# A gather-and-accumulate loop: every fourth expert value row is weighted and added on VectorE instead of on TensorE

## What is computed

```
u = take(w_u, expert)                       # [token, 128, 1024]
h = einsum('cd,ced->ce', x, u)              # one dot product of 1024 for each expert
a = gelu(h) * gate
y = einsum('ce,ced->cd', a, take(w_v, expert))   # weighted sum of 128 value rows
```

## Time and profile before

| what | value |
|---|---|
| time, median of 3 runs (lowest, highest) | 3867.13 us (3861.45, 3872.97) |
| profiled execution, first to last instruction | 3889.2 us |
| TensorE busy | 3225.7 us (83%) |
| VectorE busy | 2469.6 us (64%) |
| GpSimd busy | 2306.0 us (59%) |
| ScalarE busy | 471.7 us (12%) |
| HBM read / written | 1222.33 MB / 15.73 MB |
| mean granted TensorE clock | 0.973 |

### The profile page before, as it was taken

One profiled execution on the slowest core, in us unless ns is written; L12 is line 12 of the kernel. 1 busy time (PEld: TensorE's weight loads), 2 busy tenths in 40 slices (PEclk: granted clock), 3 DMA queues, 4 the chain that ended last, 5 costly groups with the idle time before them and its releaser, 6 DMA issues.

```text
span 3889.2 us, 35666 instructions
## 1 busy us (share of the span) xinstructions
PE 3225.7 (83%) x9848; PEld 1705.4 (44%) x9848; DVE 2469.6 (64%) x5900; ACT 471.7 (12%) x810; POOL 2306.0 (59%) x2075
## 2 busy tenths in 40 slices
PE   6999968698899887798999886887998986766676
PEld 3456744254564453354564552344664542222222
DVE  5143068478776677578765686577665885577654
ACT  1121011021111110021110010121111110000000
POOL 4000017765666767766566667655667667776775
PEclk9999989999999999999999999998999999999999
DMA  4135449998999999998999999988999999999998
GB/s 169 77 103 168 152 158 349 358 342 305 344 385 382 373 359 348 353 335 303 358 379 378 366 344 348 356 318 307 369 380 375 384 336 353 364 343 346 327 365 301
DMA packets 350437, 1240.65 MB, mean 319 GB/s; under 512 B 38480, under 2 KB 46160, under 8 KB 349712
## 3 DMA queue, kind: packets, MB, share of 16 engines
q0 software_dynamic: 294912, 1073.87, 74.7%
q1 hardware_dynamic: 34096, 117.94, 8.3%
q10 hardware_dynamic: 21216, 46.40, 3.4%
HBM read 1222.33 MB, written 15.73 MB: 318 GB/s over the span
## 4 chain that ended last, share of the span: by engine, by line
PE 40%; DMA 19%; issue 14%; DVE 12%; POOL 8%; DVEq 6%; another core or an unknown queue 1%; ACT 0%; POOLq 0%; SPq 0%
PE acc L592 17%; DMA rows<-in_peer_v,ids_peer 14%; PE fA L513 5%; DMA rows<-in_peer_u,ids_peer 5%; POOL rows L299 4%; POOL rows L309 4%; PE fB L525 3%; DVE rows L853 3%; DVE diag L864 2%; PE fA L473 2%; PE m L361 2%; PE m L557 1%; PE acc L579 1%; PE fA L536 1%; PE fB L536 1%
## 5 line engine op out<-in xcount | busy, mean ns | idle before, releaser
L592 PE MATMUL acc<-rows,diag 128*128 128x512 f32 x4096 | 1995.6, 620 | 539.2 <-DMA rows<-in_peer_v,ids_peer 468.7
L853 DVE CUSTOM_DVE_ANT_0 rows<-rows,hh 128x1024 f32<-128x1024 f32 x1024 | 1240.4, 1222 | 711.9 <-DMA rows<-in_peer_u,ids_peer 657.7
L299 POOL DMA_INDIRECT rows<-in_peer_u,ids_peer x1024 | 1108.4, 1082 | 889.9 <-DVE ids_peer L833 351.0
L309 POOL DMA_INDIRECT rows<-in_peer_v,ids_peer x1024 | 1149.5, 1123 | 534.5 <-issue 284.0
L592 PEld LDWEIGHTS acc<-rows,diag 128*128 128x128 f32 x4096 | 745.6, 194 | 1570.5 <-DMA rows<-in_peer_v,ids_peer 790.8
L864 DVE TENSOR_SCALAR diag<-ident,act_out,gate_peer 128x128 f32<-128x128 f32 x1024 | 283.6, 366 | 0.5 <-ACT act_out L1072 0.5
L557 PE MATMUL m<-hT_g,wring 128*128 128x256 f32 x1024 | 237.4, 386 | 1.1 <-ACT hT_g L1043 1.1
L513 PE MATMUL fA<-hT_g,wring 128*128 128x256 f32 x1024 | 231.2, 380 | 0.0
L557 PEld LDWEIGHTS m<-hT_g,wring 128*128 128x128 f32 x1024 | 198.9, 195 | 55.4 <-issue 29.1
L513 PEld LDWEIGHTS fA<-hT_g,wring 128*128 128x128 f32 x1024 | 195.3, 191 | 47.2 <-issue 23.0
L1072 ACT ACTIVATE act_out<-dots 128x8 f32<-128x8 f32 x128 | 26.7, 209 | 1052.5 <-DVE dots L853 705.5
(11 more groups left out here) (149 smaller groups left out, 2072.3 us busy)
## 6 DMA issues: line engine op xcount, KB each, us to landing
wring<-in_wstream SPq DMA_DIRECT2D x192, 512.0 KB
ln<-in_dft_seq ACTq DMA_DIRECT2D x32, 512.0 KB, 3.7
rows<-in_peer_u,ids_peer POOLq DMA_INDIRECT x1024
rows<-in_peer_v,ids_peer POOLq DMA_INDIRECT x1024
hT_g<-in_x SPq DMA_DIRECT2D x8, 512.0 KB, 3.7
hres_spill<-KT ACTq DMA_DIRECT2D x8, 512.0 KB, 2.7
hT_spill<-rows ACTq DMA_DIRECT2D x1, 4096.0 KB
wring<-in_wstream SPq DMA_DIRECT2D x16, 256.0 KB
```

Source lines behind the costliest of these rows:

```text
L299: pool.indirect_dma_start(u_rows[:, i % NU, :], None, peer_u, bass.IndirectOffsetOnAxis(ap=ids_peer[:, t, s:s + 1], axis=0)).then_inc(u_in ...
L309: pool.indirect_dma_start(v_rows[:, i % NV, :], None, peer_v, bass.IndirectOffsetOnAxis(ap=ids_peer[:, t, s:s + 1], axis=0)).then_inc(v_in ...
L592: last = mm(acc[:, half * 512:(half + 1) * 512], diag[:, i % NDIAG, :], v_rows[:, i % NV, half * 512:(half + 1) * 512], start=i % SLOTS == ...
L853: v.tensor_tensor_reduce(out=row, in0=row, in1=h1_peer[:, t, :], scale=1.0, scalar=0.0, op0=ALU.mult, op1=ALU.add, accum_out=dots[:, b, i ...
```

## The change

Of every four slots, the last one (slot number mod 4 equal to 3, which is always the fourth buffer of the v ring) no longer goes to TensorE. VectorE waits for its row to land and adds coefficient times row to an SBUF tile `yvec`; the first such slot of a tile writes `yvec` instead of adding. The coefficients (activation times gate) of a batch's two such slots come from one small multiplication in `diags`, which writes six diagonal matrices instead of eight. GpSimd's v gather of such a slot waits on a semaphore of VectorE (`v_added`) instead of TensorE's. `finish` adds `yvec` to the tile's result with one more instruction after it has freed `acc`.

```diff
+VEC = 4
+PE_BATCH = BATCH - BATCH // VEC
+PE_STEPS = STEPS - STEPS // VEC
...
             def gather_v(g, i):
                 g, i = slot_of(g, i)
-                pool.wait_ge(v_free, g * STEPS + i + 1 + NDIAG - NV)
+                if i % VEC == VEC - 1:
+                    pool.wait_ge(v_added, g * (STEPS // VEC) + i // VEC + 1)
+                else:
+                    pool.wait_ge(v_free, g * PE_STEPS + pe_slots(i) + 1)
...
                 if i % SLOTS == 0:
                     pe.wait_ge(acc_free, g * TILES + i // SLOTS + 1)
+                if i % VEC == VEC - 1:
+                    return
                 if i % BATCH == 0:
-                    pe.wait_ge(diag_done, g * STEPS + i + BATCH)
+                    pe.wait_ge(diag_done, g * PE_STEPS + pe_slots(i) + PE_BATCH)
...
+            def add_row(g, i):
+                g, i = slot_of(g, i)
+                if i % VEC != VEC - 1:
+                    return
+                dve.wait_ge(v_in[i % NV], g * (16 * STEPS // NV) + 16 * (i // NV + 1))
+                c = coef[:, i // BATCH % 2, i % BATCH // VEC:i % BATCH // VEC + 1]
+                if i % SLOTS == VEC - 1:
+                    v.tensor_scalar(yvec[:, :], v_rows[:, i % NV, :], c, None, ALU.mult).then_inc(v_added, 1)
+                else:
+                    v.scalar_tensor_tensor(out=yvec[:, :], in0=v_rows[:, i % NV, :], scalar=c, in1=yvec[:, :],
+                                           op0=ALU.mult, op1=ALU.add).then_inc(v_added, 1)
...
-                dve.wait_ge(v_free, g * STEPS + BATCH * k + BATCH)
+                if positive(g * PE_STEPS + PE_BATCH * (k - 1)):
+                    dve.wait_ge(v_free, NV - 1 + g * PE_STEPS + PE_BATCH * (k - 1))
                 t, s0 = divmod(k * BATCH, SLOTS)
+                v.tensor_tensor(coef[:, k % 2, :], act_out[:, k % 2, VEC - 1:BATCH:VEC],
+                                gate_peer[:, t, s0 + VEC - 1:s0 + BATCH:VEC], ALU.mult)
                 for s in range(BATCH):
-                    v.tensor_scalar(diag[:, (k * BATCH + s) % NDIAG, :], ident[:, :], act_out[:, k % 2, s:s + 1],
+                    if s % VEC == VEC - 1:
+                        continue
+                    v.tensor_scalar(diag[:, pe_slots(k * BATCH + s) % (2 * PE_BATCH), :], ident[:, :], act_out[:, k % 2, s:s + 1],
                                     gate_peer[:, t, s0 + s:s0 + s + 1], ALU.mult, ALU.mult).then_inc(diag_done, 1)
...
                                        op0=ALU.mult, op1=ALU.add).then_inc(acc_free, 1)
+                dve.drain()
+                v.tensor_tensor(ybuf[:, :], ybuf[:, :], yvec[:, :], ALU.add)
...
             def peer(g, m, last):
                 if has_slot(g, m + LEAD + AHEAD, last):
                     dot(g, m + LEAD + AHEAD)
+                if has_slot(g, m + LEAD, last):
+                    add_row(g, m + LEAD)
```

More of the change, by code:

```diff
@@ L44 @@
 NDIAG = 2 * BATCH
+VEC = 4
+PE_BATCH = BATCH - BATCH // VEC
+PE_STEPS = STEPS - STEPS // VEC
+assert NV == VEC
 NW = 4
@@ L95, in layer_program @@
         hT_g = sb("hT_g", [P, KD, GROUP])
-        diag = sb("diag", [P, NDIAG, P])
+        diag = sb("diag", [P, 2 * PE_BATCH, P])
         ln = sb("ln", [P, 4, D])
@@ L104, in layer_program @@
         ybuf = sb("ybuf", [P, D])
+        yvec = sb("yvec", [P, D])
         ident = sb("ident", [P, P])
@@ L128, in layer_program @@
         act_out = sb("act_out", [P, 2, BATCH])
+        coef = sb("coef", [P, 2, BATCH // VEC])
         st = sb("st", [P, 3, 12])
@@ L212, in layer_program @@
         v_in = [sem(f"v_landed{i}") for i in range(NV)]
-        u_free, v_free, acc_free = sem("u_free"), sem("v_free"), sem("acc_free")
+        u_free, v_free, v_added, acc_free = sem("u_free"), sem("v_free"), sem("v_added"), sem("acc_free")
         act_done, diag_done = sem("act_done"), sem("diag_done")
@@ L232, in has_slot, with pe_slots @@
             return i < STEPS and not (isinstance(g, int) and g < 0) or i >= STEPS and not last
+        def pe_slots(i):
+            return i - i // VEC
         def used(g, c):
@@ L331, in tr @@
                 return nc.tensor.transpose(out_, in_, ident[:, :])
-            for _ in range(NDIAG):
+            for _ in range(NV - 1):
                 pe.nop().then_inc(v_free, 1)
@@ L587, in peer @@
                     pe.wait_ge(acc_free, g * TILES + i // SLOTS + 1)
+                if i % VEC == VEC - 1:
+                    return
                 if i % BATCH == 0:
-                    pe.wait_ge(diag_done, g * STEPS + i + BATCH)
+                    pe.wait_ge(diag_done, g * PE_STEPS + pe_slots(i) + PE_BATCH)
                 pe.wait_ge(v_in[i % NV], g * (16 * STEPS // NV) + 16 * (i // NV + 1))
                 for half in range(2):
-                    last = mm(acc[:, half * 512:(half + 1) * 512], diag[:, i % NDIAG, :],
+                    last = mm(acc[:, half * 512:(half + 1) * 512], diag[:, pe_slots(i) % (2 * PE_BATCH), :],
                               v_rows[:, i % NV, half * 512:(half + 1) * 512],
-                              start=i % SLOTS == 0, stop=i % SLOTS == SLOTS - 1)
+                              start=i % SLOTS == 0, stop=i % SLOTS == SLOTS - 2)
                 last.then_inc(v_free, 1)
@@ L634, in _ @@
                 dve.nop().then_inc(u_free, 1)
+            dve.nop().then_inc(v_added, 1)
             dve.nop().then_inc(acc_free, 1)
@@ L870, in finish @@
                 dve.wait_ge(stored, 16 * (g * TILES + t) + 16)
-                dve.wait_ge(v_free, g * STEPS + NDIAG + (t + 1) * SLOTS)
+                dve.wait_ge(v_free, g * PE_STEPS + NV - 1 + (t + 1) * pe_slots(SLOTS))
                 v.scalar_tensor_tensor(out=ybuf[:, :], in0=h1_peer[:, t, :], scalar=ALPHA, in1=acc[:, :],
                                        op0=ALU.mult, op1=ALU.add).then_inc(acc_free, 1)
+                dve.drain()
+                v.tensor_tensor(ybuf[:, :], ybuf[:, :], yvec[:, :], ALU.add)
                 dve.drain()
```

## The result

The changed kernel takes 3900.52 us in the median (3893.46 to 3910.36), the kernel before 3870.05 us in the runs beside it. The two medians are 30 us apart; the ratio of the runs, by which all kernels are compared here, is 1.0097, interval 1.0053 to 1.0141, so 38 us slower (21 to 55), where 24 us faster was forecast.

A forecast was written before the change was run, and what follows sets the result against it. TensorE was taken to pace gate, merge and output alone and share attention, with transfers near their limit and GpSimd's gathers filling the rest; -30 - 10 + 5 + 14 + 0 - 3 = -24 from 3867 gives 3843 us, range 3795 to 3915.

The forecast's parts named there:

- Which stages TensorE sets: TensorE alone sets the pace in gate, merge and output, shares it in attention, and doesn't in about 60% of slots.
- What it removes and adds: Whole kernel: TensorE 440 us less; VectorE about 270 us more net, with adds taken at 1.25 us each.
- Gate, merge and output, 30 us gained: These stages in three groups: gate step falls from 3.47 to 3.28 us, transfers then limit; 30 us gained, ends 7 and 60.
- What of VectorE's work lies on the path: Stage by stage, VectorE's added work mostly hidden: 5 us lost in attention with retrieval, 14 in top-k, nothing without front work.
- attention with retrieval: Attention beside the second tile's retrieval: TensorE's relief and VectorE's burden nearly cancel, 5 us lost; ends 25 lost, 30 gained.
- top-k: First tile's top-k, steps 157 to 221: added rows mostly hidden in waits for u rows, 14 us lost, ends 0 and 60.
- steps without front work: Steps after the query projections and the last group: nothing gained or lost, slot again 2.99 us.
- idle, so covered: Steps without front work: VectorE's 37% idle in the last group covers the added work and its waits for value rows.
- Rival 3: Attention with retrieval and top-k: VectorE becomes the bound, its late lumps stopping GpSimd's gathers; 3895 to 3919 us, chance 0.20.
- the point that I set for it: Rival 3 decides once the net 1.0 us of VectorE's work per added row finds no wait to fill.
- The adds hold up GpSimd: Rival 4, where GpSimd is 95% occupied: each add delays a gather by up to 1.25 us; 3948, half 3895; chance 0.05.
- 30 + 10 + 3 us: Gains booked: 30 us in gate, merge and output, 10 in attention's first part, 3 net at the end.

The follow-up runs named there:

- x_pe_frees: Changed kernel, but TensorE frees every fourth slot's buffer without matmul and VectorE neither waits nor adds (that part of the sum left out): 3825.19 us, ratio 0.9909.
- xf_filler: x_pe_frees with two zero-matrix matmuls on TensorE in place of every fourth slot's work: 3817.49 us, ratio 0.9893 of the kernel before.
- g_gate: Kernel before, with VectorE adding only the 16 rows a group due in the gate, merge and output stages (steps 72 to 135): 3868.20 against 3888.62 us, ratio 0.9952.
- y_dve_waits: Changed kernel, but VectorE only waits for every fourth slot's row and frees the buffer, without adding: 3840.33 us, ratio 0.9947 of the kernel before.
- two-input burdens: Two runs of the kernel before plus a 1.28 us VectorE instruction with two SBUF inputs at every fourth step: ratios 1.0213 and 1.0190.
- one-input: Two runs of the kernel before plus a VectorE maximum with one SBUF input (1.22 us) at every fourth step: ratios 1.0134 and 1.0142.
- w_two: Second run of the kernel before plus a 1.28 us VectorE instruction with two SBUF inputs at every fourth step: 3943.75 against 3877.81 us, ratio 1.0190.
- b_again: The kernel before, unchanged, run once more for a second trace: span 3895.3 us.
- w_one: Second run of the kernel before plus a 1.22 us VectorE maximum with one SBUF input at every fourth step: 3931.96 against 3877.81 us, ratio 1.0142.
- z_filler: Changed kernel plus two zero-matrix matmuls on TensorE at every fourth slot, restoring its amount of work: 3906.68 us, ratio 1.0125 of the kernel before.
- d_six: Kernel before, but VectorE writes six of a batch's eight diagonal matrices; TensorE keeps all matmuls, using a neighbour's matrix: 3852.78 against 3879.03 us, ratio 0.9946.
- xd_eight: xf_filler with VectorE writing eight matrices a batch again, the two extra to a spare tile: 3888.52 against 3877.81 us for the kernel before, ratio 1.0028.

## Why the prediction was wrong, step by step

- *Which stages TensorE sets*: right for gate and merge. The output projection itself takes 47 us instead of 49 from its first to its last start, but the query projections start no earlier behind it.
- *What it removes and adds*: right in size for VectorE. Adds at 1.28 us (1.25 taken), VectorE 264 us more (270), its waits for value rows 45 us in all. Wrong for TensorE, 220 us less instead of 440: what is left of its work runs at a lower clock. x_pe_frees is busy 2994 us; xf_filler without its filler's 501 us has the same work in 2718.
- *Gate, merge and output, 30 us gained*: half of it or a little more. The step fell to 3.39 us (1035.6 to 1188.1 less 3.2, over 44 steps), not 3.28; 15 us by the stages' table, 19 by g_gate's time, 23 by the u gathers of steps 72 to 136 (219.4 and 220.2 us before, 212.0 after, three groups).
- *What of VectorE's work lies on the path*: this is the step that failed, by its size. I charged 5 us for attention with retrieval, 14 for top-k and nothing for steps without front work, 19 us for 270 us of work, 0.07 us per us. (2 us per 120 over 3.5 x 205 us are 12, not 14, so the sum was -26.) The runs give 0.18 (from y_dve_waits to the changed kernel, 58 for 318), 0.22 to 0.26 (two-input burdens), 0.17 and 0.18 (one-input), 0.32 (taking work away). In the traces y_dve_waits and the changed kernel are 48 us apart, 47 of them in the steps with retrieval: 21 beside attention (161.0 to 168.1 us a group), 13 in top-k (184.0 to 188.2) and 13 in the last group's steps 27 to 123 (292.2 to 304.8). The burdens grew the same three by 13, 32 and 7 us. So the price is about 0.4 us per us in these steps (52 us for 99 instructions of 1.28) and nothing outside them, at 51% and 67% busy. The argument "idle, so covered" held where it was made of idle steps. What it got wrong is how much a VectorE at about 80% hides in attention and in top-k, and the last group: I read it as one window with VectorE at 63%, and 96 of its steps hold the second tile's retrieval, with VectorE at 72% and the others at 51%.
- *Rival 3*, given 0.20 and 3895 us, is nearest to what happened, in its mechanism and in its signs: a slot in top-k takes 3.38 us (above 3.3) and one in attention with retrieval 3.86 us (above 3.8), as the two windows below show. Beside attention the point that I set for it is met: VectorE waits for u rows for 1 us of 494 before. In top-k it is not, 68 and 73 us of such waits stood there, and the burdens still cost 32 us; GpSimd's waits for dots there grow from 41 and 38 us to between 60 and 79. Part of top-k's length is the clock's (x_pe_frees against xf_filler, 187.5 and 179.0 us a group for steps 157 to 212). That its 3895 us lies so close to 3900.52 is partly luck: it holds 33 us for TensorE's relief, and nothing for the clock or for the last group's retrieval.

```profile
922.00:1036.00 114.00, 84.13 (x278) 46.66 (x277) 98.61 (x215) 22.16 (x30) 62.08 (x59) 0.82 0.85 299
1364.00:1494.00 130.00, 101.36 (x292) 60.72 (x293) 111.09 (x292) 16.26 (x33) 84.18 (x77) 0.86 0.94 342
```

- *The adds hold up GpSimd*, given 0.05: shown as a mechanism, and perhaps a part of the cost, about 15 of the 74 us of w_two by the runs' ratios. For the adds themselves no run gives a price; x_pe_frees, which has none, has gathers of 2310 us in sum, as long as the changed kernel's 2302. I dismissed it on one row, a gather of 0.94 us beside a dot. That gather started 0.14 us before the dot; it was first. The tally over the trace speaks the other way, 1.37 us against 0.94. The Trainium skill, SBUF — State Buffer, section "SBUF: two separate sides", says that the one which starts first holds the shared port pair and the other waits to the end of the instruction: by that rule, the traces agree for instructions with two SBUF inputs. The same page names an instruction in a 2-port mode as another holder; if the diagonal matrices, float32 with one tensor input, run in such a mode, their 0.99 us does not show it. The float32 copy of 128x1024 from SBUF to SBUF (hh, 0.71 us) does hold up gathers: the nine that start in its course in before, b_again, changed, w_two and w_one take 1.2 us in the mean.
- *TensorE's clock* was missing from the sum. Its granted clock is a share of 2.4 GHz and has the two levels 2.4 and 1.2; a slot's four records take 1.98 us at the one and 3.78 us at the other in the last group. x_pe_frees against xf_filler: 225 us less busy time, and no time gained. With it the 30 + 10 + 3 us that I booked for TensorE's relief were worth about nothing together. In the changed kernel the query stage is held long by both at once: it is 206 us with the clock restored (z_filler), and 207 without VectorE's burden (x_pe_frees).

```profile
3537.86 3.78 PE L607 MATMUL acc<-rows,diag 128*128 128x512 f32 x4 [2.88 <-DMA rows<-in_peer_v,ids_peer]
...
3552.54 1.98 PE L607 MATMUL acc<-rows,diag 128*128 128x512 f32 x4 [1.18 <-DMA rows<-in_peer_v,ids_peer]
```

These are two slots of the changed kernel 15 us apart; the clock granted is 0.50 around the first and 1.00 around the second, and TensorE had stood idle before both.

The sum after the fact: x_pe_frees -35 us (of which 21 are the matrices that VectorE no longer writes, d_six), the wait in order and later release +15, the adds +58. That is +38, as it must be, since these are the differences between neighbours on the way from the one kernel to the other. Set against the forecast: TensorE's side was to give 43 us, the net 10 of attention among them, and gave about 14 (35 less 21; nothing, if the matrices weigh the 52 us of xf_filler and xd_eight), VectorE's was to cost 19 and cost 52 (58 + 15 - 21). So 33 of the 62 us missed lie with VectorE's price and 29 with TensorE's relief, which the clock ate.

## What to carry to other kernels

When one in-order engine frees the buffers of a gather stream, its mean idle share says little: measure what a us of its work costs by adding and taking away a little, and look for where it costs. Here it was 0.2 to 0.3 us per us over the whole kernel at 64% busy, about 0.4 in the steps in which that engine was 78% busy with a second kind of work between the gathers, and nothing in the steps at 51%. A window that mixes such steps hides this. Work is moved best only in the stages where the engine that gives it is full; the same adds in the gate and output stages alone gave 0.5%. An engine that loses work may be granted a lower clock in its other stages, and a single row that goes against a mechanism proves nothing until the rows like it are counted.

## What had not been expected of the hardware

- A gather issued by GpSimd takes 0.94 us beside an idle VectorE and 1.37 us in the mean under a dot, a VectorE instruction with two SBUF inputs (748 of 2009 gathers), 0.96 us under one of the same length with one input (94 gathers). It is held up only if the VectorE instruction started first.
- TensorE, 83% busy before and 77% after, is granted 0.973 and 0.896 of its clock in the mean, and 0.80 to 0.84 in the stages in which it works in single slots with waits between, where the kernel before has 0.98. Zero-matrix matmuls in place of the work taken away bring it back to 0.97 (xf_filler; 0.954 in the mean in z_filler).
- ScalarE writes a 128x128 diagonal matrix in 0.39 us beside 0.37 us on VectorE, and at 21% busy no engine is recorded as waiting for one of them: moving all of them is worth 2.1%.
